# Attention values as fp32 products with the exponentials stationary, and masks added by the vector engine

## The reference, cut to what matters

```python
s_c = jnp.einsum('bkgqd,bknd->bkgqn', qc, k_cmp) - slopes5 * d_c
p_c = masked_softmax(s_c, d_c >= 0)
o_c = jnp.einsum('bkgqn,bknd->bkgqd', p_c, v_cmp)
...
p_s = masked_softmax(s_s, (d_s >= 0))
o_s = jnp.einsum('bkgqm,bkqmd->bkgqd', p_s, vs)
...
m_w = (d_w >= 0) & (d_w < WINDOW) & (w_pos[None, :] >= 0)
p_w = masked_softmax(s_w, m_w)
o_w = jnp.einsum('bkgqm,bkmd->bkgqd', p_w, vw)
return gc[..., 0:1] * o_c + gc[..., 1:2] * o_s + gc[..., 2:3] * o_w
```

## Time and profile before

| | |
|---|---|
| Median of 3 runs | 1502.29 us |
| Profiled execution | 1510.79 us |
| Its span | 1509.1 us |
| Instructions in it | 17457 |
| Second pass, first key/value head | 357.0 to 465.0 us of the span |
| Second pass, second key/value head | 548.0 to 658.7 us of the span |

### The profile page before, as it was taken

One profiled execution on the slowest core, in us unless ns is written; L12 is line 12 of the kernel. 1 busy time (PEld: TensorE's weight loads), 2 busy tenths in 40 slices (PEclk: granted clock), 3 DMA queues, 4 the chain that ended last, 5 costly groups with the idle time before them and its releaser, 6 DMA issues.

```text
span 1509.1 us, 17457 instructions
## 1 busy us (share of the span) xinstructions
PE 1446.8 (96%) x6670; PEld 1149.7 (76%) x6670; DVE 741.4 (49%) x900; ACT 447.5 (30%) x626; POOL 109.0 (7%) x74
## 2 busy tenths in 40 slices
PE   7999999999897998989999999999999999999995
PEld 6788888876565765668888888888888888888874
DVE  6333512395664965655344435344443535444456
ACT  5211201404786046843232111212112121111211
POOL 0011000000111002110001000101000010100000
PEclk9999999699997999999999999999999999999997
DMA  5111120000000030011102111111111111111102
GB/s 203 55 56 56 39 94 21 9 1 3 1 1 7 1 115 1 1 56 57 50 23 68 43 56 42 56 42 56 42 42 56 56 42 42 56 49 35 56 0 111
DMA packets 18686, 67.62 MB, mean 45 GB/s; under 512 B 2088, under 2 KB 2856, under 8 KB 18472
## 3 DMA queue, kind: packets, MB, share of 16 engines
q1 hardware_dynamic: 18396, 66.03, 12.8%
q0 software_dynamic: 240, 0.93, 0.3%
HBM read 63.01 MB, written 4.19 MB: 45 GB/s over the span
## 4 chain that ended last, share of the span: by engine, by line
PE 89%; DVE 4%; issue 2%; POOL 2%; ACT 1%; DMA 1%; DVEq 0%; SPq 0%; ACTq 0%; POOLq 0%
PE PS L321 18%; PE PS L322 18%; PE PS L325 18%; PE PS L1222 5%; PE PS L1226 5%; PE PS L1223 5%; PE PS L1031 3%; PE PS L1032 2%; PE PS L1127 2%; PE PS L1129 1%; PE PS L1128 1%; PE PS L1108 1%; PE PS L1109 1%; DVE nmax L782 1%; PE PS L1013 1%
## 5 line engine op out<-in xcount | busy, mean ns | idle before, releaser
L321 PE MATMUL PS<-R,wh 128*128 128x512 f32 x1200 | 471.5, 393 | 13.5 <-DVE wl L313 11.4
L322 PE MATMUL PS<-R,wh 128*128 128x512 f32 x1200 | 469.0, 391 | 0.0
L325 PE MATMUL PS<-R,wl 128*128 128x512 f32 x1200 | 371.3, 391 | 0.0
L321 PEld LDWEIGHTS PS<-R,wh 128*128 128x128 f32 x1200 | 226.8, 189 | 61.7 <-DVE wl L313 11.9
L322 PEld LDWEIGHTS PS<-R,wh 128*128 128x128 f32 x1200 | 226.8, 189 | 47.7 <-issue 0.7
L325 PEld LDWEIGHTS PS<-R,wl 128*128 128x128 f32 x1200 | 226.4, 189 | 47.4
L306 ACT ACTIVATE wh<-raw 128x1024 fp32r<-128x1024 f32 x97 | 101.8, 1050 | 260.6 <-PE PS L1226 174.0
L919 DVE TENSOR_TENSOR F<-PS,F 128x1024 f32<-128x1024 f32 x88 | 107.6, 1223 | 92.0 <-PE PS L1226 92.0
L1222 PE MATMUL PS<-R,wh 128*128 128x512 f32 x352 | 137.0, 389 | 1.1 <-DVE wl L313 1.1
L1223 PE MATMUL PS<-R,wh 128*128 128x512 f32 x352 | 136.9, 389 | 0.0
L834 DVE TENSOR_TENSOR wl<-raw,wh 128x512 fp32r<-128x512 f32 x148 | 102.7, 697 | 60.2 <-ACT raw L578 58.5
(11 more groups left out here) (142 smaller groups left out, 1416.6 us busy)
## 6 DMA issues: line engine op xcount, KB each, us to landing
raw<-in_w_units SPq DMA_DIRECT2D x97, 512.0 KB, 3.4
F<-in_xT SPq DMA_DIRECT2D x16, 512.0 KB, 8.5
outT<-F SPq DMA_DIRECT2D x8, 512.0 KB, 3.1
F<-in_w_cmp SPq DMA_DIRECT2D x1, 2048.0 KB, 7.9
masks<-in_masks POOLq DMA_DIRECT2D x1, 448.0 KB, 5.0
R<-in_alibi_q POOLq DMA_DIRECT2D x2, 160.0 KB, 4.5
R<-R SPq DMA_DIRECT2D x4, 48.0 KB
R<-in_alibi_k POOLq DMA_DIRECT2D x1, 136.0 KB, 3.5
```

What stands on the lines that cost most here:

```text
L321: nc.tensor.matmul(out, w_h, hi(kt)[:, cols], start=first, stop=False)
L322: nc.tensor.matmul(out, w_h, lo(kt)[:, cols], start=False, stop=False)
L325: last = nc.tensor.matmul(out, w_l, hi(kt)[:, cols], start=False, stop=end)
```

## The change

The second pass is rewritten.

- `values(s)`: the exponentials are no longer split. One tile `EB` (fp32) of 128 keys and 4 x 128 queries is the stationary operand, 128 columns for each head, and V (fp32, 65 columns) is the moving one. So 4 fp32 products replace 3 fp32r matmuls of 512 columns. The output has queries in partitions; all 12 of a query tile (3 branches, 4 heads) lie in two banks, and two pairs of banks (4, 5 and 6, 7) alternate. `turn`, the copies and the transposes are gone, and DVE reads the outputs in PSUM.
- ACT takes one exponential a step; DVE makes no residuals, and V isn't split and lies in `PBm`.
- The masks of the second pass are added by DVE in PSUM (`mask_tile`), 28 tiles for each `g`, before ACT's exponential. They are stored transposed; those of the compressed branch come by a transfer of their own on GpSimd's queue. The large negative number is -2^100.
- The loops over `g` are written out on all engines.
- The load of unit 24 waits for the last `pv_done`; after the second head TensorE doesn't wait for the last `o_scaled`.

```diff
@@ constants
-NEG = -1e30
+NEG = -2.0 ** 100
@@ tiles
-        VH = piece(NV * VW).rearrange("p (j d) -> p j d", d=VW)
-        VL = piece(NV * VW).rearrange("p (j d) -> p j d", d=VW)
+        MH, ML, CM = piece(P), piece(P), piece(T)
+        V = PBm[:, :, :].rearrange("p a b -> p (a b)")[:, 0:NV * VW].rearrange("p (j d) -> p j d", d=VW)
+        def mask_of(s):
+            i, br, j = STEPS[s]
+            if br == 2:
+                return f32(CM[:, i * P:(i + 1) * P])
+            if j == i:
+                return masks[:, M_TILES:M_TILES + P]
+            return masks[:, M_TILES + P:M_TILES + 2 * P] if br == 1 and j == i - WT else None
+        def outputs(i):
+            return PS[:, 4 + 2 * (i % 2):6 + 2 * (i % 2), 0:6 * VW].rearrange("p a (n d) -> p a n d", d=VW)
@@ SyncE
-            sp.wait_ge(pt_lo, KV * NS)
+            sp.wait_ge(pv_done, KV * NS)
             load(sp, 24, 0, 0, 0)
@@ GpSimd
+            pool.dma_start(CM, cmp_masks_d).then_inc(cm_in, 16)
-            with pool.Fori(0, KV) as g:
+            for g in range(KV):
@@ ACT, second pass
+                for s in range(NS):
+                    act.wait_ge(st_ready, NS * g + s + 1)
+                    if mask_of(s) is not None:
+                        act.wait_ge(masked, masked_upto(g, s))
+                    if s > 3:
+                        act.wait_ge(pv_done, NS * g + s - 3)
+                    nc.scalar.activation(EB[s % 4], PS[:, s % 4, :], ACT.Exp).then_inc(e_ready, 1)
@@ DVE, second pass
+                def mask_tile(s):
+                    mask = mask_of(s)
+                    if mask is None:
+                        return
+                    dve.wait_ge(st_ready, NS * g + s + 1)
+                    scores = PS[:, s % 4, :].rearrange("p (h q) -> p h q", h=GROUP)
+                    nc.vector.tensor_tensor(scores, scores, mask.rearrange("p (o q) -> p o q", o=1)
+                                            .broadcast_to([P, GROUP, P]), ALU.add).then_inc(masked, 1)
+                mask_tile(0)
+                mask_tile(1)
+                for s in range(NS + 1):
+                    if s + 2 < NS:
+                        mask_tile(s + 2)
+                    if s in TILE_ENDS:
+                        weigh(TILE_ENDS.index(s))
@@ TensorE
-            with pe.Fori(0, KV) as g:
+            for g in range(KV):
...
-                    if mask is not None:
-                        last = nc.tensor.matmul(out, masks[:, mask:mask + P], masks[:, M_ID:M_ID + GROUP * P],
-                                                start=False, stop=True)
...
-                    nc.tensor.matmul(out, VH[:, n, 0:DH + 1], PTH[s % 4], start=first, stop=False)
-                    nc.tensor.matmul(out, VL[:, n, 0:DH + 1], PTH[s % 4], start=False, stop=False)
-                    nc.tensor.matmul(out, VH[:, n, 0:DH + 1], PTL[s % 4], start=False, stop=end).then_inc(pv_done, 1)
+                    if first and br == 0 and i > 1:
+                        pe.wait_ge(o_scaled, TT * g + i - 1)
+                    pe.wait_ge(e_ready, NS * g + s + 1)
+                    n = (0, TT, 2 * TT)[br] + j
+                    for h in range(GROUP):
+                        number = GROUP * br + h
+                        a, b = divmod(number, 6)
+                        last = nc.tensor.matmul(outputs(i)[:, a, b, 0:DH + 1], EB[s % 4][:, h * P:(h + 1) * P],
+                                                V[:, n, 0:DH + 1], start=first and number % 6 == 0,
+                                                stop=end and number % 6 == 5)
+                    last.then_inc(pv_done, 1)
...
-                pe.wait_ge(o_scaled, TT * g + TT)
+                pe.wait_ge(o_scaled, TT * g + (TT if g == 0 else TT - 1))
```

More of the change, by code:

```diff
@@ L189, in f32, with masked_upto @@
             return ap.bitcast(F32)
+        def mask_of(s):
[5 more added lines that the diff above has]
+            return masks[:, M_TILES + P:M_TILES + 2 * P] if br == 1 and j == i - WT else None
+        def masked_upto(g, s):
+            tiles = [n for n in range(NS) if mask_of(n) is not None]
+            return len(tiles) * g + sum(n <= s for n in tiles)
+        def outputs(i):
+            return PS[:, 4 + 2 * (i % 2):6 + 2 * (i % 2), 0:6 * VW].rearrange("p a (n d) -> p a n d", d=VW)
         consts_in, late_in, w1_in, ak_in = sem("consts_in"), sem("late_in"), sem("w1_in"), sem("ak_in")
-        masks_in, params_in = sem("masks_in"), sem("params_in")
+        masks_in, params_in, cm_in, masked = sem("masks_in"), sem("params_in"), sem("cm_in"), sem("masked")
         g_hi, g_lo, r_ready, conv_ready, tapr_ready = (sem("g_hi"), sem("g_lo"), sem("r_ready"), sem("conv_ready"),
@@ L364, in hybrid_layer @@
         ENDS = [s + 1 for s in range(NS) if s + 1 == NS or STEPS[s + 1][:2] != STEPS[s][:2]]
-        STEP_OF_TURN = [ENDS[3 * i + 2] + 2 for i in range(TT)]
+        TILE_ENDS = [ENDS[3 * i + 2] for i in range(TT)]
         def act_at(par, e, part):
@@ L523, in _ @@
                                  ACT.Exp, scale=-1.0).then_inc(gexp_ready, 1)
-            act.wait_ge(clear_ready, 5)
+            act.wait_ge(clear_ready, 4)
             act.wait_ge(unit_lo, N_IN + 1)
-            with act.Fori(0, KV) as g:
+            for g in range(KV):
                 def kv_rows(what, half):
@@ L572, in _ @@
[L572 to L586, removed]
+                nc.scalar.activation(V[KCMP:KCMP + NCMP, 2 * TT, 0:DH], CMP_OUT[1][0:NCMP, 0:DH], ACT.Copy).then_inc(kc_hi, 1)
@@ L749, in _ @@
             nc.vector.tensor_copy(posb[:, :], PS[:, 7, BANK // 2:BANK // 2 + 2]).then_inc(posb_ready, 1)
-            with dve.Fori(0, KV) as g:
-                steps.enter(g, KV, 2 * TT)
+            for g in range(KV):
                 for half in range(2):
@@ L1006, in _ @@
             pe.wait_ge(ak_in, 16)
-            pe.wait_ge(clear_ready, 5)
-            with pe.Fori(0, KV) as g:
+            pe.wait_ge(clear_ready, 4)
+            for g in range(KV):
                 def compressed_hidden(kv, src, pairs=range(CMP_BLOCK // 2)):
@@ L1145, in _ @@
                 key_scores(2)
[L1146 to L1148 removed]
+                pe.wait_ge(v_ready, g + 1)
+                pe.wait_ge(kc_hi, 3 * g + 3)
+                for s in range(NS):
                     if s + 3 < NS:
                         key_scores(s + 3)
[L1151 to L1155 removed]
+                    values(s)
+                pe.wait_ge(o_scaled, TT * g + (TT if g == 0 else TT - 1))
             order = [4, 5, 6, 7, 0, 1, 2, 3]
```

138 lines of the change are left out of this document (42 added, 96 removed).

## The result

The changed kernel takes 1658.30 us (median of four executions, 1654.58 to 1662.96); the kernel before took 1501.93 us in the same comparison (four, 1501.45 to 1505.12). The ratio is 1.1038, with a 95% interval of 1.1004 to 1.1071: slower by a tenth. The profiled execution of the changed kernel is 1654.58 us, that of before 1510.79 us. So the direction was right and the time lies in the range, but the forecast (A, 1564 us) missed by 94 us: the loss is more than twice the one forecast. The time is that of rival B, both second passes at half clock.

A forecast was written before the change was run, and what follows sets the result against it. TensorE was taken to bound most of the second pass. Gains of 5.9 + 8.6 + 7.0 + 4.6 = 26.1 us gave 1476 us at full clock; one pass at half clock adds 88: 1564 us, range 1466 to 1660.

The forecast's parts named there:

- A: Likeliest case: one of the two second passes stays at half clock, 1564 us, chance 0.42.
- rival B: Both second passes stay at half clock, 1654 us, chance 0.24.
- The step at full clock: Second pass, new step: two score matmuls and eight load-and-matmul pairs on TensorE, 1.352 us, 74 steps a pass.
- A pass that stays low: A second pass left at half clock takes 2.57 us a step, +88 us for each such pass.
- The pitch of a pair: Value products: each fp32 product is two load-and-matmul pairs, 0.112 us apart at full clock, paced by the weight load.
- jump back of its loop: Between the heads: TensorE stands 7.54 us for its loop's jump; unrolling, the stretch gains 7.0 us.
- C: Neither second pass stays at half clock, 1476 us, chance 0.32.
- Masks and exponentials hidden: Second pass: DVE's mask additions (0.7 us) and ACT's exponentials (0.6 us) hide behind TensorE, scored three steps ahead.
- hold whichever clock they find: fp32 pairs neither raise nor lower TensorE's clock, so a pass entered at half clock may stay there.
- the very first masked tile is not hidden: 0.4 us: Start of a second pass: the first tile's mask and exponential aren't covered by TensorE work, costing 0.4 us.
- each pass draws anew: Whether the entry burst of eight score matmuls lifts the clock depends on how fall and burst lie, each pass.
- 6 in 10: Chance given for each second pass to stay at half clock, the two not quite independent.

The follow-up runs named there:

- before_unrolled: The kernel before with its loop over the two heads written out on all engines, nothing else changed: 1497.77 us, ratio 0.9918.
- filled_table: The changed kernel with 12 wide matmuls in TensorE's wait ahead of each second pass and the exponential's table loaded early: 1481.22 us, ratio 0.9821.
- more_filled: filled_table with 11 more matmuls behind head 0's pass and 9 behind the second head's 32 pairs, into unread banks: 1478.40 us, ratio 0.9807.
- late_burst: The changed kernel with 20 more 512-column matmuls once per second pass, ahead of step 24 of 74: 1548.48 us.
- gap_new: filled_table with one idle of TensorE put into each second pass, waiting for GpSimd to clear a buffer three times: 1547.44 us.
- filled_both: The changed kernel with 12 score-shaped matmuls in TensorE's wait for the maxima ahead of each second pass: 1568.46 us, ratio 1.0415.
- table_first: The changed kernel with a single-element exponential on ACT so its table loads before the mask wait: 1571.86 us; repeated, median 1571.35 us, ratio 1.0424.
- long_burst: The changed kernel with 16 more 512-column matmuls behind the wait for the maxima, ahead of each pass's eight score matmuls: 1661.36 us.
- one_pass_values: The changed kernel with exponentials and V as single fp32r pieces, each value product one pair instead of two, low parts left out: 1529.23 us.
- filled_head0: The changed kernel with 12 score-shaped matmuls in TensorE's wait for the maxima, ahead of head 0's second pass only: 1570.40 us.
- gap_old: before_unrolled with one idle of TensorE put into each second pass, waiting for GpSimd to clear a buffer three times: 1503.92 us.

## Why the prediction was right or wrong

*The terms.* The step at full clock: 1.352 us forecast, 1.37 us measured. At half clock: 2.57 and 2.56 us. The pass at full clock and with nothing lost at the start: 100.4 us, measured 101.1 us; at half clock 190.3 us, measured 190.0 and 189.6 us. A pass that stays low: +88 us, measured 88.9 us (190.0 - 101.1). The pitch of a pair: right, and the same for 65 and 66 columns; that the load sets it fits that, but wasn't tried. Between the heads 11.2 us, measured 11.6 us; at the end 13.1 us, measured 13.2 us. Its "jump back of its loop": right, by before_unrolled. The sum for a kernel with no pass down (C, 1476 us) is met by filled_table within 6 us and by more_filled within 3 us. Masks and exponentials hidden: right in the traces, where TensorE waits for exponentials 0.5 us in the changed kernel and 1.3 us in filled_table. That the masks alone cost nothing wasn't tried by itself.

*The row that spoke for the mechanism.* That pairs "hold whichever clock they find" came from one stretch at 0.50 and one at 1.00. late_burst, gap_new and filled_both bear it out for the mix, as long as TensorE has no gap: it held 1.00 for a pass of 101 us in filled_table and 0.50 for 190 us in the changed kernel. The fall at the entry was read a little too early: the passes of the kernel before began at full clock (0.51 us at 356.95) and lost it in their first matmuls, not in the wait itself.

*The step that failed* is "the very first masked tile is not hidden: 0.4 us", and with it "each pass draws anew". I priced that start as time and left it out of the argument on the clock. I summed mask and exponential there and didn't ask where ACT's table load would go, though the trace of before shows it at 355.68, in the wait for the transfer. It moved behind the mask, and the burst of eight matmuls, on which the draw hung, ended in an idle TensorE. As time it is indeed 0.3 us at half clock; as a break behind the burst it went with the loss of every pass in the four executions. Without it the forecast's case appears with its time (table_first, five of seven). The forecast had one pass down; the second, 88.9 us, is what this step missed. Thus the chance of 6 in 10 for a pass to stay low was about right for a kernel without the gap (9 of 14 passes), and far too low for this one: B came out in all four executions. The chances didn't follow from the 6 in 10 either: 0.42 for one pass and 0.24 for both mean 0.42 / 2 + 0.24 = 0.45 for a pass; 6 in 10, drawn independently, is 0.36 for B, 0.48 for A and 0.16 for C.

*The rule of the skill.* By the Trainium skill (TensorE: Matmul & The Clock Gate, Why this matters for your kernels) keeping TensorE continuously busy gets it to full rate. The measurement decides against it here: TensorE was busy for 189.66 of 190.00 us and stayed at 0.50. The time of the rival that went by the rule (C) was met only when 512-column matmuls and an early table load kept the clock from falling.

## What to carry to other kernels

Ask of a new inner loop not only what it costs at full clock, but whether it can climb back from half clock: here a pass took 101 us at the one level and 190 us at the other, and its predecessor 108 us. Look at every start of such a loop for idle time of TensorE, at the order wait for input, first burst, first dependent result, and see that one-time work of another engine (a table load) is issued before that engine's first wait and not behind it. Where idle time must remain, a dozen wide matmuls into a free PSUM bank can fill it; here they and one early table load turned a kernel of ratio 1.10 into one of 0.98.

## What the runs showed of the hardware that was not expected

The table load stands directly ahead of the first activation that needs it and behind that activation's wait: 1.28 us at 354.38 in the changed kernel, at 355.68 without a wait in the one before. A single-element activation moves it (352.09 in filled_table, before any wait of the pass).

Idle time of TensorE of 1.35 to 1.46 us inside full-clock work was followed by a fall some 0.5 to 2.5 us later in four places (filled_both's second head, both heads of long_burst, one_pass_values's first head), but not in two others (the first heads of filled_both, 1.46 us up to 360.56, and of filled_head0, 1.46 us up to 360.67, where the pass behind it stayed at 1.00). One of 2.71 us in gap_old's second head brought none either. So a gap of that size may cost the clock and need not.

One fp32r product of 66 columns takes as long as one of the two parts of an fp32 product of 65: 0.21 us at half clock. So a matmul with its load, of an eighth of a score matmul's columns, costs half of its 0.43 us.

With the idle stretches between the heads filled too (more_filled), four executions lie within 0.2 us; the seven of the kernel before beside them lie within 11.2 us, and those of the changed kernel, in another comparison, within 8.4 us. That the spread of such a kernel is the clock's is likely by that, but not shown.
